# The arena of on-chip pieces begins 128 bytes further on in a two-block transformer kernel

## The reference

```python
x = first_block(x, mem, positions, w_in, ...)            # 2 layers
return second_block(x, p_2, norm_mix_g_2, w_in_2, ...)   # 2 layers

# first_block, each layer
h = x @ w_in[l]                       # 1024 -> 7328 columns, split in 8
o_mla, o_diff, o_mem = three attention branches
merged = sum(g[i] * (o[i] @ w_branch part i))
x = layernorm(ALPHA * x + merged @ w_out[l])
x = layernorm(ALPHA * x + square(relu(x @ mlp_w1[l])) @ mlp_w2[l])

# second_block, each layer
s = split(rmsnorm(h) @ w_in[l])       # 1024 -> 14912 columns
y_ssd, y_hg, y_ml = three recurrent branches
h = h + sum(gate[i] * (y[i] @ w_br[i])) @ w_out[l]
up = dwconv(rmsnorm(h) @ w_up[l])     # 1024 -> 5632
h = h + (silu(a_half) * v_half) @ w_down[l]
h = h + (p[l] @ w_ple[l]) * sigmoid(h @ w_ple_gate[l])
```

## Time and profile before

| | before |
|---|---|
| median of 3 runs | 2476.61 us |
| the runs | 2473.0, 2476.61, 2489.43 us |
| span of the profiled execution | 2475.0 us |
| TensorE busy | 2427.1 us, 98% |
| VectorE busy | 1771.3 us, 72% |
| ScalarE busy | 1463.7 us, 59% |
| GpSimd busy | 286.6 us, 12% |

### The profile page before, as it was taken

The page is one execution under the profiler, slowest core; times in us unless marked ns, Lnnn a source line. Parts: engine busy times, 40 slices in busy tenths (PEclk is TensorE's granted clock), DMA queues, the critical chain, the costliest instruction groups (busy, mean ns, idle before and its releaser), DMA issues.

```text
span 2475.0 us, 43073 instructions
## 1 busy us (share of the span) xinstructions
PE 2427.1 (98%) x17744; PEld 2224.3 (90%) x17744; DVE 1771.3 (72%) x2813; ACT 1463.7 (59%) x2162; POOL 286.6 (12%) x222
## 2 busy tenths in 40 slices
PE   8999999999999999899999999999999999999998
PEld 8888999888889899799999799998899999899996
DVE  4568675565586755678778887885588668887875
ACT  5547555545475455477656655664677656556654
POOL 0000002000000000002123710000012207500000
PEclk9999999999999999999999999999999999999999
DMA  7554476655545566555566645665555657645664
GB/s 254 154 145 125 151 253 193 204 182 163 145 118 153 175 196 196 173 155 137 152 194 194 196 134 185 196 198 189 142 161 143 172 174 206 182 152 187 192 209 128
DMA packets 358919, 430.49 MB, mean 174 GB/s; under 512 B 20616, under 2 KB 286310, under 8 KB 358468
## 3 DMA queue, kind: packets, MB, share of 16 engines
q1 hardware_dynamic: 341312, 401.72, 53.7%
q10 hardware_dynamic: 14340, 14.93, 2.6%
q0 software_dynamic: 3072, 11.10, 1.5%
HBM read 424.44 MB, written 3.24 MB: 173 GB/s over the span
## 4 chain that ended last, share of the span: by engine, by line
PE 91%; DVE 5%; ACT 2%; issue 1%; DMA 1%; POOL 0%; POOLq 0%; ACTq 0%; DVEq 0%
PE ps L112 89%; PE ps L115 2%; DVE wlo L121 1%; ACT lnv L118 0%; DMA kT<-in_diff_lambda 0%; DVE sbc L130 0%; DVE hgQ L121 0%; ACT L118 0%; DMA memN<-in_mem 0%; DVE kT L121 0%; DVE sz L130 0%; DVE xN L130 0%; DVE hgA L148 0%; DVE ple L121 0%; ACT E L118 0%
## 5 line engine op out<-in xcount | busy, mean ns | idle before, releaser
L121 DVE TENSOR_TENSOR wlo<-wring,whi 128x1024 fp32r<-128x1024 f32 (+1 forms) x768 | 920.6, 1219 | 261.8 <-ACT whi L118 261.4
L118 ACT ACTIVATE whi<-wring 128x1024 fp32r<-128x1024 f32 (+1 forms) x768 | 803.3, 1054 | 425.1 <-PE ps L112 409.7
L112 PE MATMUL ps<-uT,whi 128*128 128x256 f32 x4640 | 817.8, 280 | 6.1 <-DVE wlo L121 4.4
L112 PEld LDWEIGHTS ps<-uT,whi 128*128 128x128 f32 x4640 | 705.4, 188 | 16.2 <-DVE wlo L121 7.3
L112 PE MATMUL ps<-uT,wlo 128*128 128x256 f32 x2320 | 645.4, 278 | 0.0
L112 PEld LDWEIGHTS ps<-uT,wlo 128*128 128x128 f32 x2320 | 436.4, 188 | 0.0
L112 PE MATMUL ps<-xT,whi 128*128 128x256 f32 x2112 | 376.3, 282 | 2.2 <-DVE xT L121 1.1
L112 PEld LDWEIGHTS ps<-xT,whi 128*128 128x128 f32 x2112 | 321.4, 188 | 9.1 <-issue 5.2
L112 PE MATMUL ps<-xT,wlo 128*128 128x256 f32 x1056 | 294.4, 279 | 0.0
L112 PE MATMUL ps<-whi,hid 128*128 128x512 f32 x864 | 269.4, 391 | 0.0
L112 PEld LDWEIGHTS ps<-xT,wlo 128*128 128x128 f32 x1056 | 198.5, 188 | 0.3
(11 more groups left out here) (392 smaller groups left out, 3561.2 us busy)
## 6 DMA issues: line engine op xcount, KB each, us to landing
wring<-in_w_in SPq DMA_DIRECT2D x346, 512.0 KB, 4.1
wring<-in_mlp_w SPq DMA_DIRECT2D x128, 512.0 KB, 4.5
wring<-in_w_up SPq DMA_DIRECT2D x88, 512.0 KB, 4.5
wring<-in_w_down SPq DMA_DIRECT2D x44, 512.0 KB, 4.4
wring<-in_w_branch SPq DMA_DIRECT2D x32, 512.0 KB, 3.4
wring<-in_w_out SPq DMA_DIRECT2D x32, 512.0 KB, 4.3
wring<-in_mem_w_kv SPq DMA_DIRECT2D x16, 512.0 KB, 6.5
wring<-in_w_br_hg SPq DMA_DIRECT2D x16, 512.0 KB, 4.8
```

The costliest lines, as they stand in the source:

```text
L112: return self.e.matmul(*p, **k) if self.e else Nothing()
L118: return self.e.activation(*p, **k) if self.e else Nothing()
L121: return self.e.tensor_tensor(*p, **k) if self.e else Nothing()
```

## The change

The base of the arena is computed otherwise: before, it is the first byte past the fixed tensors that is 64 above a multiple of 128; now it is the first that is 192 above a multiple of 256.

```diff
-    base = (nc.sbuf_base + 63) // 128 * 128 + 64
+    base = (nc.sbuf_base + 63) // 256 * 256 + 192
     K.ar = Arena(nc, base, (nc.sbuf_usable_end - base) // 4 // 64 * 64)
```

## The result

The change makes the kernel slower: 2516.23 us (median of 4 runs, 2511.87 to 2520.46) against 2477.73 us, ratio 1.0155 with a 95% interval of 1.0133 to 1.0177, some 38 us. The prediction, 2476.6 us and no change, is wrong, and its range (to 2499 us) doesn't hold the time. The two profiled executions lie 43.6 us apart, somewhat more than the medians; the one of after is the slowest of its four runs.

What follows compares the result with a forecast made beforehand. The prediction took TensorE, mostly its fp32r products, as the bound: 2475.0 us profiled plus 0 for all terms, plus 1.6 us to the median, gave 2476.6 us, no change (0.86), range 2463 to 2499 us.

Steps and rivals of the forecast that it cites:

- The two paces of 256 columns: TensorE's 256-column products: 113.3 or 117.9 ns between starts, set when a stream starts and kept throughout it.
- the bit worth 128 bytes: Operand addresses: distances of 256 and 512 bytes don't matter, only 128 is untested; its term taken as 0.
- the first rival: TensorE's matmuls: the new place puts more streams in the slow pace, at worst 34 us, 2511 us; chance 0.10, shared with a third pace.
- last sign of being wrong: Windows on uT in the profile after: the forecast is wrong if nearly all show the same count of records.
- for that bit there is one small witness: Products on cq, operand roles swapped: 121 ns in one layer, 115 in the other, so both paces stay open; term 0.
- The term for 512 columns: 512-column products: 912 aligned ones losing their place, bound +2.1 us; the other 2340 or so could gain 5.4 us.
- a pace that the trace doesn't have: Rival: pieces 128 from whi, or 64 above it in 512 columns, cost 9 ns more, +29 us, 2506 us; within a shared 0.10.
- All slow: +32 us: Bound for 256-column products: 7060 quick matmuls all going slow at 4.6 ns each.
- The clock: Stretches at granted clock 0.50: one more or less is 1 to 4 us, nothing on the mean, wider range.
- The share of slow streams: 256-column products: some 0.4 slow, from a mean record of 278 ns, so 4700 slow against 7060 quick.
- The page of the Trainium skill: TensorE's two independent read ports: by it no relative place of operands costs anything, term exactly 0.

Runs made afterwards that it cites:

- e7: Arena base 256 bytes above that of e3, so again at remainder 0 by 256: 2524.9 us, 1.0182 of the kernel before.
- e5: Separate kernel, TensorE alone: both product forms on eight pieces 0 to 224 bytes above the rings' place, six starts each; one execution, 256 columns at 64: 116.3 ns.
- e3: Kernel before with the arena base 64 bytes earlier, remainder 0 by 256, 128 away from whi: 2526.8 us, ratio 1.0211.
- e4: Kernel before with the arena base 64 bytes further, remainder 128 by 256, distance 0 to whi: 2532.8 us, ratio 1.0232.
- e10: Kernel before with the constants allocated between whi and wlo, so wlo lies at remainder 0 by 256: 2475.7 us, 0.9956 of before on the same chip.
- e8: e5 with places 144, 176, 184, 192, 200, 208, 240 and 16, ten starts each: 256 columns 114.3 ns at 192, 120.0 and 120.2 eight bytes beside.

## Why the prediction was wrong

**What held.** TensorE's pace was the only way in which the change could act; no wait, DMA or other engine took a part that shows (VectorE and ScalarE within 1 us). The two paces of 256 columns, that a stream keeps the pace that it starts with, and that only the bit worth 128 bytes was untested while 256 and 512 make no difference, were read correctly (e7, and the one table from the whole kernels). The mechanism was on the list as the first rival, with 2511 us at most and a chance of 0.10; the median went 5 us past that worst case, for the 512-column reason below. The prediction's last sign of being wrong, nearly all windows on `uT` with the same count, is what came.

**The step that failed: "for that bit there is one small witness".** I took the products on `cq` as showing that the new order of the two operands leaves both paces open, and from that a term of 0. That both are open is true (two streams of six at 64 in e5), but nothing followed for the share, and the share was the whole question: of the 11,856 products, some 7300 ran quick before and some 860 after, and that alone is +29 us where the sum had 0. The witness was 36 matmuls in two streams, each of which had one start; two starts can't tell five in six from two in six. After the change `cq` shows the same two paces the other way round, 113.6 ns in the first layer and 117.8 in the second, while the rest of the kernel has gone slow. It also has the roles swapped at 256 columns, and e3 and e4 show that the two forms don't follow one rule: of the four distances tried there, 0 is the best for 512 columns and the worst for 256. A known sensitivity (2.3 ns for 64 bytes) with one bit untested should have been priced by its bound, with the slow case at a third or more of the chance.

**The term for 512 columns was mis-sized.** The bound was +2.1 us, for 912 aligned products that would lose 2.3 ns. Measured: +13.5 us over all 3251, the mean of undisturbed starts going from 228.7 to 233.1 ns: 64 above `whi` costs 233.3 where 192 costs 229.4, and 128 away costs 232.7 where 0 costs 227.0. The rival "a pace that the trace doesn't have" named exactly these two places and guessed 9 ns; they are 3.9 and 5.7 ns above before.

**The bound on 256 columns came out by luck to the microsecond.** "All slow: +32 us" was worked out from the earlier trace rows, and +32.3 us was measured, but only 29 us of it are pace: some 860 matmuls stayed quick, and the clock of that execution made up the difference. The clock, which the prediction priced at 1 to 4 us a stretch with nothing on the mean, is +3.5 us there.

**The share of slow streams** was taken as 0.4 from means of 278 ns; counted by threes it was a third (some 3700 of 11,100).

**The page of the Trainium skill** that was weighed ("TensorE: Matmul & The Clock Gate", Part 2: two independent read ports, and a weight load that takes nothing from the running matmul) gave exactly 0. The runs differ: with no other engine at work, the distance by 256 bytes between the loaded columns and the moving ones sets the distance between starts anywhere from 113.3 to 120.2 ns (256 columns) and from 226.7 to 234.2 (512). The measurement decides.

**Open.** Which banks or lines of SBUF stand behind the table was not shown, nor why `oE` and `oD` kept their pace after the change and `yT` never had the quick one before; that goes by how a stream starts, which was varied but not explained. Where most of the 11 us of e10 come from is open as well. Distances finer than 8 bytes, other places of `whi` in the finer table, and an arena 256 bytes above that of before weren't tried, the latter for want of room.

## What to carry to other kernels

When TensorE is the bound and runs fp32r products back to back, the addresses of the two operands are a tuning parameter by themselves (here 1.6% for 128 bytes, 2.3% at the worst place): write down each operand's address by 256 bytes, and allocate so that a later tensor added in front can't move one group against another. A small kernel of streams on differently placed pieces, with several starts each, gives the table of paces in one run. It is no substitute for the big kernel: for e10 it foretold -14 and +3 us for the two forms where the traces of the big kernel showed -10 and +8. Where a trace shows a price for an attribute in one value of several, an untested value gets its bound and a real chance, and not the benefit of a witness with two samples.

## What the runs showed of the hardware

- fp32r matmuls with their weight loads, at a granted clock of 1.00 (2.4 GHz): 113.3 ns for 256 columns and 226.7 ns for 512 at best (one part in 16 more than 256 or 512 periods of 2.4 GHz); at unlucky places up to 120.2 and 234.2 ns.
- The best distance of an activation from `whi` is 192 by 256 when the activation moves (256 columns), exact to 8 bytes (114.3 ns, and 120.0 and 120.2 beside it), and 0 or 240 when the activation is loaded (512 columns, 227.7 and 227.5 ns). The pattern repeats after 256 bytes (e3 and e7).
- At a distance of 192 or 64 a stream has one of two paces, 113.3 or 117.8 ns, from its start on and for as long as it goes, up to 1031 matmuls here. The distance changes how many starts end in the quick one: five of six (e5) and eight of ten (e8) at 192, two of six at 64, ten of ten near it (113.3 to 114.5 ns) with `wlo` 128 from `whi`.
- ScalarE, VectorE and panel loads at work beside TensorE changed none of the 16 paces by more than 0.02 ns.
